# Query and key tiles of the first layer's mixer, projected as two half tiles in turn

## What is computed

```
u = rmsnorm(h, norm_mix_pre)
proj = u @ w_in
q_na, k_na, v_na, q_gl, k_gl, v_gl, g_gl, z_gl = parts
o_na = neighbourhood_attention(q_na, k_na, v_na, rpb)     # 8 heads of 64
o_gl = gla_bidirectional(q_gl, k_gl, v_gl, g_gl, z_gl, ...)  # 4 heads, chunks of 64
mix = concatenate([rmsnorm(o_na), o_gl]) @ w_o
h = h + rmsnorm(mix)
```

## Time and profile before

| | |
|---|---|
| median of 3 runs | 1904.34 us (1903.39 to 1904.81) |
| span of the profiled execution, first to last instruction | 1902.2 us |
| TensorE busy with matmuls / weight loads | 1761.9 us (93%) / 1517.4 us (80%) |
| VectorE, ScalarE, GpSimdE busy | 1020.4 us (54%), 650.3 us (34%), 88.4 us (5%) |
| mean granted TensorE clock | 0.973 |

### The profile page before, as it was taken

How to read it: one execution, slowest core, us unless ns; L and a number is a source line. 1 busy time by engine, 2 the same in 40 slices (tenths; PEclk the granted TensorE clock), 3 DMA queues, 4 the chain that set the end, 5 groups by cost and what they waited for, 6 DMA issues and landing times. The chain is left out here.

```text
span 1902.2 us, 38594 instructions
## 1 busy us (share of the span) xinstructions
PE 1761.9 (93%) x17168; PEld 1517.4 (80%) x17168; DVE 1020.4 (54%) x1527; ACT 650.3 (34%) x1067; POOL 88.4 (5%) x115
## 2 busy tenths in 40 slices
PE   6998999889999999999999988887589999999998
PEld 5888877889979979897777777777468887888877
DVE  3235675555735636557664455654656535353554
ACT  3243244533433423433333333332244312121232
POOL 7000000010000000100000000000002000000020
PEclk8999999989999999979999999999889999999999
DMA  5211120211222222312222100000052222222221
GB/s 165 89 68 45 56 89 23 90 45 67 89 103 92 94 89 89 111 64 88 78 95 73 56 14 4 5 4 9 4 230 89 92 107 89 91 97 100 89 89 67
DMA packets 29132, 144.57 MB, mean 76 GB/s; under 512 B 6315, under 2 KB 9659, under 8 KB 14380
## 3 DMA queue, kind: packets, MB, share of 16 engines
q1 hardware_dynamic: 24828, 133.58, 19.7%
q0 software_dynamic: 3856, 7.87, 1.5%
q10 hardware_dynamic: 288, 0.73, 0.1%
HBM read 134.82 MB, written 8.91 MB: 76 GB/s over the span
## 5 line engine op out<-in xcount | busy, mean ns | idle before, releaser
L228 DVE TENSOR_TENSOR w_w_lo<-w_w_raw,w_w_hi 128x2048 fp32r<-128x2048 f32 x66 | 151.2, 2292 | 182.5 <-ACT w_w_hi L215 182.1
L240 PE MATMUL f_bank<-u_hi,w_w_hi 128*128 128x258 f32 x704 | 202.5, 288 | 6.7 <-DVE u_lo L1481 4.2
L241 PE MATMUL f_bank<-u_hi,w_w_lo 128*128 128x258 f32 x704 | 201.3, 286 | 0.0
L242 PE MATMUL f_bank<-u_lo,w_w_hi 128*128 128x258 f32 x704 | 199.9, 284 | 0.0
L240 PE MATMUL g_bank<-g_y_hi,g_w_hi 128*128 128x512 f32 x384 | 151.2, 394 | 17.0 <-DVE g_w_lo L228 12.7
L241 PE MATMUL g_bank<-g_y_hi,g_w_lo 128*128 128x512 f32 x384 | 150.2, 391 | 0.0
L242 PE MATMUL g_bank<-g_y_lo,g_w_hi 128*128 128x512 f32 x384 | 150.2, 391 | 0.0
L215 ACT ACTIVATE g_w_hi<-g_w_raw 128x2048 fp32r<-128x2048 f32 x45 | 85.9, 1909 | 167.7 <-PE g_bank L242 165.5
L240 PEld LDWEIGHTS f_bank<-u_hi,w_w_hi 128*128 128x128 f32 x704 | 134.2, 191 | 8.0 <-issue 7.2
L215 ACT ACTIVATE w_w_hi<-w_w_raw 128x2048 fp32r<-128x2048 f32 x66 | 125.8, 1906 | 32.0 <-PE f_bank L242 32.0
L242 PEld LDWEIGHTS f_bank<-u_lo,w_w_hi 128*128 128x128 f32 x704 | 135.0, 192 | 0.0
(11 more groups left out here) (516 smaller groups left out, 3948.7 us busy)
## 6 DMA issues: line engine op xcount, KB each, us to landing
g_w_raw<-in_w_ff SPq DMA_DIRECT2D x32, 1024.0 KB, 4.8
w_w_raw<-in_w_in SPq DMA_DIRECT2D x30, 1024.0 KB, 4.8
w_w_raw<-in_w_ffn_in SPq DMA_DIRECT2D x22, 1024.0 KB, 4.8
w_w_raw<-in_w_ffn_out SPq DMA_DIRECT2D x12, 1024.0 KB, 4.8
w_w_raw<-in_w_o SPq DMA_DIRECT2D x4, 1024.0 KB, 5.0
gate_pre<-rw_t POOLq DMA_DIRECT2D x16, 256.0 KB, 2.3
g_w_raw<-in_w_up SPq DMA_DIRECT2D x4, 1024.0 KB, 9.0
g_branch<-gate_pre SPq DMA_DIRECT2D x4, 1024.0 KB, 12.3
```

The lines of the kernel that those rows point to most:

```text
L228: nc.vector.tensor_tensor(R.lo[:, r, 0:size], R.raw[:, r, 0:size], R.hi[:, r, 0:size].bitcast(F32), ALU.subtract).then_inc(R.split, 1)
L240: nc.tensor.matmul(out, w_hi, u_hi, start=start, stop=False)
L241: nc.tensor.matmul(out, w_lo, u_hi, start=False, stop=False)
L242: return nc.tensor.matmul(out, w_hi, u_lo, start=False, stop=stop)
```

## The change

Each feature-major tile becomes two units of 24 products: first all 24 products of 272 columns into bank 6, then all 24 of 256 columns into bank 7. Each unit has its own `tile_done`, its own ScalarE copy and its own `tile_free`. `FM` counts units and is 16; the ring phase of the four query and key slots counts 4 units per slot. A unit's first product waits for the copy of the unit before the last one, the one that used the same bank. The number of products, their operands and the number of ScalarE copies (8 times L929, L930 and the last one) stay as they were. `issued` (44, 20, 6, ...) is unchanged.

```diff
-        FM, TM = 8, 10
+        FM, TM = 16, 10
         TILES = FM + TM
-        length = [48] * FM + [24] * TM
+        length = [24] * TILES
...
-            return (fm_na.n0 + g // 2, g % 2) if g < FM else (tm_na.n0 + (g - FM) // 5, (g - FM) % 5)
+            return (fm_na.n0 + g // 4, g % 4) if g < FM else (tm_na.n0 + (g - FM) // 5, (g - FM) % 5)
...
-            return g % 2 == 1 if g < FM else (g - FM) % 5 == 4
+            return g % 4 == 3 if g < FM else (g - FM) % 5 == 4
...
+                    pe.wait_ge(R.tile_free, fm_na.c0 + max(g - 1, 0))
                     if g < FM:
-                        pe.wait_ge(R.tile_free, fm_na.c0 + g)
+                        part_of = slice(0, cut) if g % 2 == 0 else slice(cut, L)
+                        out = bank[:, 6, 0:cut] if g % 2 == 0 else bank[:, 7, 0:GRID // 2]
                         for k in range(KT):
-                            w = slice(k * SLOT + m * P, k * SLOT + m * P + P)
+                            w = slice(k * SLOT + m // 2 * P, k * SLOT + m // 2 * P + P)
                             for left, right in ((R.hi, u_hi), (R.lo, u_hi), (R.hi, u_lo)):
                                 start, stop = k == 0 and left is R.hi and right is u_hi, k == KT - 1 and right is u_lo
-                                nc.tensor.matmul(bank[:, 6, 0:cut], left[:, r, w], right[:, k, 0:cut], start=start, stop=stop)
-                                yield
-                                last = nc.tensor.matmul(bank[:, 7, 0:GRID // 2], left[:, r, w], right[:, k, cut:L], start=start, stop=stop)
+                                last = nc.tensor.matmul(out, left[:, r, w], right[:, k, part_of], start=start, stop=stop)
                                 if stop:
                                     last.then_inc(R.tile_done, 1)
                                 yield
                     else:
-                        pe.wait_ge(R.tile_free, fm_na.c0 + (g if g == FM else g - 1))
                         yield from token_tile(bank[0:size[m], 6 + g % 2, 0:SLOT], r, m)
...
-                        to = by_groups(acc[:, g, META:L])
-                        nc.scalar.activation(acc[:, g, 0:META], bank[:, 6, 0:META], ACT.Copy)
-                        nc.scalar.activation(to[:, 0:4], by_rows(bank[:, 6, META:cut]), ACT.Copy)
-                        nc.scalar.activation(to[:, 4:8], by_rows(bank[:, 7, 0:GRID // 2]), ACT.Copy).then_inc(R.tile_free, 1)
+                        to = by_groups(acc[:, g // 2, META:L])
+                        if g % 2 == 0:
+                            nc.scalar.activation(acc[:, g // 2, 0:META], bank[:, 6, 0:META], ACT.Copy)
+                            nc.scalar.activation(to[:, 0:4], by_rows(bank[:, 6, META:cut]), ACT.Copy).then_inc(R.tile_free, 1)
+                        else:
+                            nc.scalar.activation(to[:, 4:8], by_rows(bank[:, 7, 0:GRID // 2]), ACT.Copy).then_inc(R.tile_free, 1)
...
-                mixer = [R.phase(count, tiles) for count, tiles in ((1, 1), (2, 2), (4, 5), (4, 2), (2, 5), (2, 4), (2, 4))]
+                mixer = [R.phase(count, tiles) for count, tiles in ((1, 1), (2, 2), (4, 5), (4, 4), (2, 5), (2, 4), (2, 4))]
```

## The result

The changed kernel took 1883.08 us (median of 4 runs, 1881.82 to 1886.64) beside 1904.57 us for the kernel before (4 runs, 1903.39 to 1907.55): a ratio of 0.9892, 95% interval 0.9876 to 0.9907. That is 21.5 us faster, where 10.8 were forecast, and lies outside the range of the prediction. Over all executions of the two, these and those timed later, the medians are 1884.3 (16 executions of the changed kernel, 1878.6 to 1895.1) and 1903.4 (86 of the kernel before, 1893.1 to 1909.4, one at 4403 us left out), 19 us apart, and the means 1886.0 and 1902.3, 16 us apart. Much of what follows is about those last five to ten microseconds.

The account below looks back on a forecast made before the run. TensorE, busy for 93% of the span, was taken to bound the kernel. Stops of 9.9 us and slow second products of 0.9 us gave -10.8 us, from 1904.34 to 1893.5 us, range 1890.2 to 1897.5.

Parts of the forecast that it names:

- The waits at the tile ends: TensorE's waits for the ScalarE copy at query and key tile ends: the seven ordinary ones should go whole.
- The long one: Wait of 2.3 us at the third tile's end, behind ScalarE's exponentials: counted as gone, with room of 0.8 us.
- What a stop costs: Each tile-end stop costs 0.16 us beyond its idle time, plus 0.11 for a slow second product; together 10.8 us.
- Copies in halves: ScalarE's same 24 copies, some started earlier: costed at nothing, at most 0.3 us once.
- products in one bank: 24 products in a row into one bank, not alternating: cost nothing, bounds 0 and 3.8 us over 384.
- who is late next: VectorE's chains at group 3's scores and the scan: slack 0.3 and 0.5 us, neither should bind.
- the close places: Group 3's scores and the scan, where VectorE might bind; if both do, 0.8 us is lost.
- The clock in the stage: Clock fall at 200 us, costing 2.4 us, left as is; bounds +2.4 us if it vanishes, -3 for one more.
- Rival one: Clock stays up after the sixth tile's end too: gain 13.2 us, time 1891.1 us; chance 0.2.
- Everything later moves as a whole: Work after the changed stage is ordered by semaphores and only starts earlier; nothing in the sum for it.
- The bounds of the range: 1890.2 us (clock better, 1 us of rounding in stops and runs) to 1897.5 (part taken back, or 3 us of clock).

Follow-up runs that it names:

- stop6_back: Changed kernel, in which only the first unit of the seventh tile waits for both copies of the tile before; median 1892.5 us, ratio 0.9940 to the kernel before.
- the pair with held clocks: Changed kernel and kernel before, each with idle TensorE products filling pauses in three later places; medians 1882.7 and 1895.4 us.
- waits_back: Changed kernel, but the first unit of each tile waits for both copies of the tile before; median 1896.9 us, ratio 0.9976 to the kernel before.
- Shifts of 0.8, 1.7 and 2.5 us: Changed kernel with 7, 14 or 21 unused 256-column products ahead of the stage; medians 1893.4, 1892.0 and 1892.9 us.

## Why the prediction missed, step by step

**The waits at the tile ends: right.** The seven ordinary ones, the one before the values among them, are gone; units follow each other in 0.12 to 0.13 us. **The long one: right**, with 0.95 us of room where 0.8 were reckoned.

**What a stop costs: right in size.** The old order's four profiles have stages of 95.4, 97.1, 97.1 and 94.4 us, with 6.8, 10.2, 10.2 and 3.4 us at the lower level. Taken out at 0.41 us a us (1.4 for 3.4, from stop6_back), that leaves 92.6, 92.9, 92.9 and 93.0, on average 92.8 against 82.0: 10.8 us, as forecast. Two other ways give the same: the 82 executions of the kernel before whose clock is on record and the 16 of the changed one, brought to equal clock, differ by 10.6, the pair with held clocks by 11.1. The rule of the Trainium skill (Perfetto Trace Analysis, Tensor Engine Instruction) that the profiler models the end of a product held in the runs as well: by the idle column waits_back has 5.9 us of stops, by its stage's length 7.8.

**Copies in halves, products in one bank, who is late next: right**, all at nothing. The bounds of 3.8 us for the bank and 0.8 us for the close places were not needed.

**The clock in the stage: this step failed.** The prediction said that the fall at 200 us "comes before the stop at the sixth tile's end can have caused it", and left the clock's cost as it was. The rows showed small products since 196.85 and a clock of 0.53 in the window from 200. But the stop's gap opens with the product at 199.85 and runs to 201.25, and the clock's record puts the fall at 200.12, 0.27 us after it. A window of 2 us that begins at 200 was read as if the fall came ahead of the pause; it came inside it, by the starts of the products. By the modelled end of that product, 200.13, no idle time had yet passed, so the rows of before alone can't settle what caused the fall; stop6_back did, for there one stop alone brought it back. How so short a part of the stop can be enough is not shown. Rival one, the clock stays up as well, was right in its mechanism, and near in its 2.4 us: the stage gained 13.4 us between the first two profiles, which is 2.6 beyond the waits' 10.8, and 3.2 on average over the old order's four (their stages' mean is 96.0; 14.0 less the 10.8). A second argument fell with the first, that "seven other stops of about the same kind are passed at 1.00": in the next three profiles the 2.3 us stop was followed by a fall too. The Trainium skill (TensorE: Matmul & The Clock Gate, A second HAM failure mode) speaks of micro-idles between groups of products that make the clock oscillate. The trace agrees at two stops of eight: this one, which stands eight full products behind a run of 16 by 16 ones, and the longest. The other six of about 1 us are passed at 1.00 in every profile.

**"Everything later moves as a whole": this step failed too, and weighs more in the first comparison.** The later products stand in the same order as before, but their clock did not stay the same. From the states to the end the first profile differs by 7.8 us, where the sum had nothing. Over 82 executions of the one and 16 of the other the mean time at the lower level went from 96.7 to 83.4 us. At 0.42 that is 5.6 us on average, of which 3.2 are the stage's and 2.4 the later stages'. With the first four executions of the changed kernel alone it is about 8. The mean gain of 16 us is then 10 to 11 for the waits, about 3 for the clock in the stage and under 3 for the later clock; even this mean gain lies outside the range. The 21.5 of the first comparison has 5 us in it that four executions on either side don't average out: the changed kernel's first four had 78.1 us at the lower level, its other twelve 85.2. As far as these executions show, that part of the miss is chance and not an effect of the change.

**The bounds of the range: too narrow for the same reason.** 1 us for "rounding in stops and runs" came from three runs within 1.4 us. Executions of one and the same kernel span 16 us here.

What stays open: whether the later stages' 2.4 us on average belong to the change at all, and why the later stretches are as long as they are in one execution and half that in the next. Shifts of 0.8, 1.7 and 2.5 us all lost some 4 us against the unshifted mean (1890.4 to 1886.0), with no trend over the three; with six to ten executions of each, that the unshifted kernel is truly better placed is likely and not shown. The two kernels with stops put back, waits_back and stop6_back, stand at 97.1 and 95.2 us of lower level, as high as the kernel before (96.7), though at most 3.4 us of it lie in their stages. Whether the stop at the sixth tile would be harmless with other work than the small decay products ahead of it was not tried either.

## What to carry over

Wait for the unit before the last one, and split a tile so that each bank can be freed on its own; price a stop from product start to product start, not by the idle column. Before a stop is called harmless for the clock, look at what stands just ahead of it, and place the fall by the clock's own record rather than by a window's edge. Compare two kernels at equal granted clock, or hold the clock up in both, because a change in one stage can move later stretches by more than it gains itself, and a few runs that agree don't bound that.

## Hardware behaviour that I had not expected

- A pause of 1.1 to 1.4 us from start to start, eight full products behind a run of 16 by 16 ones, was followed by 3.4 to 6.8 us at 1.2 instead of 2.4 GHz in five of six profiles. After the six pauses of 1.1 to 1.2 us elsewhere in the stage the clock never fell.
- The one longer pause, 2.3 us of idle time behind full products, was followed by 3.4 us at 1.2 GHz in three of four profiles, the fall 1.1 to 1.5 us after TensorE had started again. After the 2.0 us one of waits_back it didn't fall.
- Once down, the clock can stay down while TensorE is busy most of the time: 35.2 of 40 us busy at a mean clock of 0.74 from 800 us on, with a stretch of 20.5 us.
- Fall and return at the same place of the program are no property of the program alone: the stretches near 390 and 800 us lasted 10.2 and 6.8 us in one execution of the changed kernel and 17.1 and 17.1 in two others.
- Idle products in the pauses went with a higher granted clock of the work behind them: 1.00 in one stage, in both kernels, where they had 0.91 and 0.74 without.
